# A hybrid sequence trunk on one core: the attention's output gate is formed in the final product, and the seams between stages are reordered

## The reference, cut to what matters

```
# end of the even layer
a_out = g * sigmoid(g @ w_glu + b_glu) * silu(g_a)        # GLU, g = gelu(y)
b_out = attention * silu(g_b)
x = x + concat([a_out, b_out]) @ ev_w_out
# odd layer
h = rmsnorm(x, norm_w[1])
q, k, v, r, a_lr = split_cols(h @ od_w_in, [512, 512, 1024, 1024, 16])
log_a = log_sigmoid(a_lr @ w_a2 + b_a) / 16
c_out = gla_mixer(q, k, v, log_a) * silu(r)               # 4 heads, chunks of 64, per-head rmsnorm
x = rmsnorm(x + c_out @ od_w_out, final_norm)
```

## Time and profile before

| | us |
|---|---|
| median of three runs | 1678.32 (1676.89 to 1682.54) |
| profiled execution, its own time | 1679.81 |
| span of the profiled execution | 1677.7 |
| TensorE busy | 1598.3 (95%) |
| VectorE busy | 976.1 (58%) |
| ScalarE busy | 750.2 (45%) |
| GpSimd busy | 448.7 (27%) |

### The profile page before, as it was taken

How to read it: one execution, slowest core, us unless ns; L and a number is a source line. 1 busy time by engine, 2 the same in 40 slices (tenths; PEclk the granted TensorE clock), 3 DMA queues, 4 the chain that set the end, 5 groups by cost and what they waited for, 6 DMA issues and landing times.

```text
span 1677.7 us, 23100 instructions
## 1 busy us (share of the span) xinstructions
PE 1598.3 (95%) x7626; PEld 1287.5 (77%) x7626; DVE 976.1 (58%) x1751; ACT 750.2 (45%) x1824; POOL 448.7 (27%) x646
## 2 busy tenths in 40 slices
PE   5999999999999989999889999996999999989998
PEld 4777788777777668888667888885788888868886
DVE  6744545667676563324476565777665666765443
ACT  6522334666666563334344343445443334442221
POOL 3883000000000341200275434345134343300110
PEclk9999999999999999999999999998999999999999
DMA  5566544455444766224367444355244343476663
GB/s 217 147 179 188 157 151 134 144 169 150 150 139 131 198 188 242 101 96 143 118 202 251 158 124 153 123 189 188 92 156 152 122 161 117 134 250 205 188 190 112
DMA packets 251388, 268.71 MB, mean 160 GB/s; under 512 B 53992, under 2 KB 186760, under 8 KB 251272
## 3 DMA queue, kind: packets, MB, share of 16 engines
q1 hardware_dynamic: 248616, 265.58, 50.5%
q10 hardware_dynamic: 2656, 1.67, 0.4%
HBM read 164.24 MB, written 102.96 MB: 159 GB/s over the span
## 4 chain that ended last, share of the span: by engine, by line
PE 71%; DVE 11%; ACT 5%; issue 5%; DMA 4%; POOL 3%; SPq 1%; DVEq 0%; ACTq 0%; POOLq 0%
PE bank L1225 22%; PE bank L2565 10%; PE bank L2623 10%; PE bank L2749 8%; PE score_banks L2565 4%; PE score_banks L2749 2%; DVE odd_stage L2300 2%; PE score_banks L1281 1%; DVE ht_lo L2242 1%; PE bank L1308 1%; DMA odd_gl_in<-scr_heads 1%; PE bank L1262 1%; DVE odd_w_lo_S L2242 1%; PE score_banks L2667 1%; PE bank L2689 1%
## 5 line engine op out<-in xcount | busy, mean ns | idle before, releaser
L1225 PE MATMUL bank<-ht_hi,ev_w_hi 128*128 128x512 f32 x576 | 239.9, 416 | 2.4 <-DVE ht_lo L937 2.4
L1225 PE MATMUL bank<-ht_hi,ev_w_lo 128*128 128x512 f32 x576 | 226.8, 394 | 0.0
L1225 PE MATMUL bank<-ht_lo,ev_w_hi 128*128 128x512 f32 x576 | 226.6, 393 | 0.0
L1225 PEld LDWEIGHTS bank<-ht_hi,ev_w_hi 128*128 128x128 f32 x576 | 109.0, 189 | 38.7 <-issue 17.1
L1225 PEld LDWEIGHTS bank<-ht_lo,ev_w_hi 128*128 128x128 f32 x576 | 108.9, 189 | 24.9
L2565 PE MATMUL bank<-ht_hi 128*128 128x512 f32 x288 | 120.1, 417 | 5.8 <-issue 5.8
L1225 PEld LDWEIGHTS bank<-ht_hi,ev_w_lo 128*128 128x128 f32 x576 | 109.2, 190 | 19.6
L712 POOL TENSOR_TENSOR ht_lo_raw<-ht_lo_raw,glu_g_first 128x512 f32<-128x512 f32 x4 | 6.4, 1642 | 415.9 <-DMA ht_lo_raw<-scr_gate_a 409.7
L2565 PE MATMUL bank<-ht_lo,ht_hi 128*128 128x512 f32 x288 | 113.2, 393 | 0.0
L2565 PE MATMUL bank<-ht_hi,ht_lo 128*128 128x512 f32 x288 | 112.7, 391 | 0.0
L2135 ACT ACTIVATE odd_gl_o<-bank 128x256 f32<-128x256 f32 x64 | 24.7, 385 | 168.6 <-DVE odd_gl_state L2361 156.0
(11 more groups left out here) (374 smaller groups left out, 4263.4 us busy)
## 6 DMA issues: line engine op xcount, KB each, us to landing
odd_w_raw<-od_w_in SPq DMA_DIRECT2D x24, 1024.0 KB, 5.8
odd_gl_in<-scr_heads SPq DMA_DIRECT2D x32, 640.0 KB, 4.8
scr_heads<-odd_stage SPq DMA_DIRECT2D x64, 256.0 KB, 6.4
...
ev_s_cos_sin<-scr_s_cos_sin SPq DMA_DIRECT2D x32, 256.0 KB
...
scr_gla_mix<-odd_gl_out SPq DMA_DIRECT2D x32, 256.0 KB, 2.3
```

The source lines that it names most:

```text
L1225: mm = pe.matmul(acc[n % 3], w[j][:, k, :], h[:, k, t], start=(k == 0 and r == 0), stop=(k == KT - 1 and r == 2))
```

## The change

- The R gate leaves the slots: the stage tiles of the columns r are stored as they are. In the final product ScalarE makes the tanh of the loaded tile, two of 128x512 into PSUM banks (`mix_tanh`), and VectorE's `gated` becomes three operations: 0.5 * o * r, then two of (tanh + 1) * that.
- Two gates a slot, from slot 3 and from slot 51, each set done in four slots; they are stored in the slot after, ahead of everything else that SyncE does there. `gate_log` moves ahead of `advance` in VectorE's slot.
- Linear attention starts at slots 14 and 61.
- T3 and T4 of the second half are lowered by VectorE.
- GLU stage: `load_att(0)` behind `load_wo(2)` and `load_g(3)`; `gate_att(0)` behind `gate_g(3)`; `upper_att(0)` and `lower_att(0)` two products later, `upper_wo` and `lower_wo` one later; `out_products` waits for attention's low part only at k = 4.
- Start of the odd layer: the split of A11 ahead of `upper_out(14)`, that of S2 ahead of `square_out(15)`; on GpSimd S1 and S2 ahead of `inverse_out(15)`, S4 and S3 behind it; VectorE lowers S2 ahead of T2 and B21 behind S3.
- End: `split_mix(0)` and `lower(0)` at the head of slot 95.

```diff
-    GLA_AT = (17, 64)
-    GATE_AT = (4, 51)
+    GLA_AT = (14, 61)
+    GATE_AT = (3, 51)
...
-        return [8 * half + s - at_ for half, at_ in enumerate(GATE_AT) if 0 <= s - at_ < 8]
+        return [8 * half + 2 * (s - at_) + n for half, at_ in enumerate(GATE_AT) if 0 <= s - at_ < 4 for n in range(2)]
...
-            if i == 0:
+            if i == 1:
                 sp.wait_ge(hb_summed, 4 * N_TB)
...
-        load_att(0)
         load_wo(0)
         load_wo(1)
         sp.wait_ge(gg_done, 4)
         sp.wait_ge(g_lo_done, 2)
         load_wo(2)
         load_g(3)
+        load_att(0)
...
-            for k in gates_at(s - 2):
+            for k in gates_at(s - 1):
                 b, h = divmod(k, GH)
                 sp.wait_ge(la_done, k + 1)
                 sp.dma_start(scr["heads"][h, 2][:, b * BLK:(b + 1) * BLK], gm[:, k % 2]).then_inc(la_stored[k % 2], 16)
...
         gate_g(1)
         gate_g(2)
+        gate_g(3)
         gate_att(0)
-        gate_g(3)
-        for m in range(NT):
+        for m in range(NT - 1):
             inverse_out(m)
...
-        def lower_second(o):
-            pool.wait_ge(h_hi_done, NP + H_SECOND.index(o) + 1)
-            g.tensor_tensor(h_lo[o], h_raw[o], h_hi[o].bitcast(F32), ALU.subtract).then_inc(h_lo_pool, 1)
-
         pool.wait_ge(wo_free, wo_free_0 + 2)
-        for o in S_ORDER:
-            weight_sum(0, o)
+        weight_sum(0, "S1")
+        weight_sum(0, "S2")
+        inverse_out(NT - 1)
+        weight_sum(0, "S4")
+        weight_sum(0, "S3")
...
-            if i == 11:
+            if i == 13:
                 upper_att(0)
...
-            if i in (5, 7, 9, 11, 13):
-                upper_wo((i - 5) // 2)
+            if i in (6, 8, 10, 12, 14):
+                upper_wo((i - 6) // 2)
...
         for m in range(NT):
+            if m == NT - 1:
+                split(0, "A11")
             if m:
                 upper_out(m - 1)
             if m == NT - 1:
-                split(0, "A11")
+                split(0, "S2")
             square_out(m)
...
+        def mix_tanh(t):
+            j = t % 2
+            act.wait_ge(mix_in[j], mix_in_0[j] + 32 * (t // 2 + 1))
+            if t == 0:
+                act.wait_ge(on_ready, on_ready_0 + n_pair)
+                act.wait_ge(state_ready, state_ready_0 + n_pair)
+            elif t == 1:
+                act.wait_ge(ot_done, ot_done_0 + n_pair)
+            else:
+                act.wait_ge(mul_done, mul_done_0 + t - 1)
+            for h in range(2):
+                s.activation(m_th[j][h].rearrange("p (k t) -> p k t", k=4), m_sil[j][:, 4 * h:4 * h + 4], ACT.Tanh, scale=0.5
+                             ).then_inc(tanh_done, 1)
...
-            if j == 0 and is_r(it - 1):
-                silu_tanh(it - 1, "C22")
-            if j == 1 and is_r(it - 1):
-                silu_tanh(it - 1, "C21")
...
+            if s_ == 94:
+                mix_tanh(0)
+            if s_ == 95:
+                split_mix(0)
             for k in {94: (0, 1), 95: (2, 3, 4), 96: (5, 6, 7)}.get(s_, ()):
-                if k == 4:
-                    split_mix(0)
...
+            if s_ == 96:
+                mix_tanh(1)
...
+            if t + 2 < NT:
+                mix_tanh(t + 2)
...
         def prepare(i):
             s = i % 2
             dve.wait_ge(exp_done, exp_done_0 + (2 * i + 2))
+            if i == 0:
+                dve.wait_ge(hb_summed, 4 * N_TB)
...
         split(0, "A11")
         residual(NT - 1)
         sum_first("T4")
+        split(0, "S2")
         lower_first("T2")
         normed_out(NT - 1)
-        split(0, "S2")
-        lower_first("B21")
         split(0, "A12")
         split(0, "S3")
+        lower_first("B21")
         lower_first("T4")
...
-            v.scalar_tensor_tensor(m_on[j][:], m_on[j][:], 0.5, m_sil[j][:], ALU.mult, ALU.mult).then_inc(mul_done, 1)
+            halved = v.scalar_tensor_tensor(m_on[j][:], m_on[j][:], 0.5, m_sil[j][:], ALU.mult, ALU.mult)
+            halved.then_inc(half_done, 1)
+            dve.wait_ge(half_done, t + 1)
+            for h in range(2):
+                dve.wait_ge(tanh_done, 2 * t + h + 1)
+                rows = m_on[j][:, 4 * h:4 * h + 4]
+                part = v.scalar_tensor_tensor(rows, m_th[j][h].rearrange("p (k t) -> p k t", k=4), 1.0, rows, ALU.add, ALU.mult)
+            part.then_inc(mul_done, 1)
...
+            for k in gates_at(s - 1):
+                gate_log(k)
             if s and step(s - 1) is not None:
                 advance(step(s - 1))
...
-            for k in gates_at(s - 1):
-                gate_log(k)
...
             for o in H_SPLIT_AT.get(s, ()):
-                if o in H_LO_DVE:
-                    lower_second(o)
+                lower_second(o)
...
+                if m % 4 == 0 and k == 4:
+                    pe.wait_ge(att_lo_done, m // 4 + 1)
```

81 lines of the change are left out of this document (18 added, 63 removed).

## The result

The changed kernel took 1669.55 us in the median of six runs (1665.93 to 1672.22), the kernel before 1678.34 (1676.89 to 1682.54). The ratio is 0.9937, with a 95% interval of 0.9919 to 0.9954: faster by 0.6%, outside the predicted range of 1634 to 1668 and a third of the forecast gain. The profiled execution took 1671.33 us with a span of 1669.4.

A forecast was written before the change was run, and what follows sets the result against it. TensorE, busy 95% of the span, was taken as the bound, so only its idle and lower-clock time could go. 8.2 + 4.5 - 2.9 - 2.4 + 2.5 + 13.8 + 5.3 = 29.0 us gave 1649 us, range 1634 to 1668.

The forecast's parts named there:

- part 4: Linear attention three slots earlier, without the R gate inside: 2.5 us gained, from 0 to 5.
- Part 3: Gates in pairs, minima waiting for stores: 2.9 us lost in the first half, 2.4 in the second; bounds none to 22.
- two rivals: Gate stores hold VectorE: landing 6.6 us everywhere, 1666 us, chance 0.17; or landing above 8.4 us, slower, chance 0.05.
- L: Landing time of a gate's store, for which VectorE's minimum waits; TensorE's stall was put at 3L - 7.8 us.
- Small waits that swap halves: In linear attention's slots, small waits of the second half move to the first, since the step's place in the slots swaps.
- Part 5: Between the halves, with linear attention over by slot 46 and T3, T4 on VectorE: 13.8 us gained, 8 to 18.
- Part 2: Start of the odd layer, splits and sums reordered: 4.5 us gained, at most 5.3, 1.8 if GpSimd's pow were slow.
- Part 6: Into the final product, from the layer's last product to the second final tile: 5.3 us gained, from 1 to 8.
- Part 1: GLU stage, output weights and last gate block ahead of attention's first block: 8.2 us gained, between 4 and 9.
- The joined distances: Distances to the parts' ends, joined by squares: 9.1 us upward in time, 7.4 downward; forecast's own range 1640 to 1660.

The follow-up runs named there:

- start_17_61: The changed kernel with the first half's linear attention at slot 17 again, the second half left at slot 61: median 1669.5 us, ratio 0.9944 to the kernel before.

## Why the prediction was wrong

**The sign of part 4 was wrong.** "The first heads' load now waits for stores of the slot just before it, hidden by the two slots until it is scanned; if that cover is gone it costs one landing, 3.4 to 6.6 us." The cover was gone at both starts, and they cost 7.0 and 7.9 us, above that range: the pauses alone were 6.7 us (1.6 of them were there before) and 4.8 us, and 1.6 and 2.4 us of lower clock followed them. The step that failed is the cover: I counted slots of TensorE between the load and its scan, and not what stood ahead of the load in SyncE's queue. At the second start the runs show it: two slots later 7.8 us of waiting are gone. At the first start the early slot is not what lost the time, since slot 17 with pairs loses 7.2 us too and with single gates 1.8; there it was the gates in pairs, behind which the last sum of halves, for which step 0 now waits too, is stored 9 us later. That SyncE's queue carries this delay is what the traces suggest, and not shown by a run. The range of part 4, 0 to 5 us of gain, held no loss, although the text had named its price.

**The pairs' cost was looked for on the wrong engine.** Part 3 and two rivals priced VectorE's wait for the landing. L had been taken at 3.4, 7 and 4 us in the first half and 3.4 in the second; it was 2.3, 6.9 and 2.3, and 3.0, 5.7 and 2.8. The sums came out near (+1.6 and +3.0 us, forecast +2.9 and +2.4), but that is partly luck: a minimum held TensorE for 1.1 us in all, and 2.2 us of the first half are the gate product's wait for the low-rank activations, which the sum did not have. And the stores that now come first on SyncE make its queue wait for VectorE. I had counted their new place as a gain and asked for no one behind them. The pairs of runs put this at 7.8 to 8.0 us in slots 3 to 16 (one kernel also starts its gates a slot earlier), most of it seen only where linear attention starts. It is the cost that no rival had, though the range was wide.

**Small waits that swap halves.** Right: 5.5 us lost in the first half, 7.4 gained in the second, 1.9 net. The runs add the reason: a start in an even slot costs a wait in each slot with one product, in either half.

**Part 5** gave 9.9 of 13.8 us. The new waits were named (T2, B21, T1: 1.4, 0.5, 3.2 us); they measured 2.8, 0 and 4.6. The term left out was the clock behind the waits that stay: behind T1's wait, 24 matmuls took 8.5 instead of 5.5 us. The cause named in the text, GpSimd's low parts of T3 and T4, is not borne out as one of its own: moving them alone is worth 0.6 us, and moving them back 0.4 to 1.8. It is the early end of linear attention that freed the stretch, by 6.4 us against start_17_61; that little more than pays for the 5.7 us that the even start in slot 14 costs in slots 17 to 44.

**Part 2** was right (4.7 for 4.5 us), its wait moved to B22's low part as said (2.9 us); GpSimd's pow took 0.55 us, at 811.75, with VectorE idle beside it, as the 4.5 us had assumed. **Part 6** gave 7.0 for 5.3: the first half-tile took 8.7 us at the pace of the weights' low parts, 8.6 foretold, and only 0.2 us and not 1.5 behind the last product. The final tiles' extra work was free, 163.4 us against 163.5.

**Part 1** gave 5.2 for 8.2 us, and in some executions nothing. The weight came in time, as said, but GpSimd's two long operations now lie beside VectorE's low parts. The prediction placed the attention product "until about 611" and priced only its own lateness.

**The joined distances.** Downward, 0.8, 0.8, 5.3, 2.5, 4.2 and 2.7 make 7.8 us by squares and not 7.4; this moves the lower end of the range by under 1 us and changes nothing else.
